# Sampled attention of a hybrid decoder step: the product with V, values held in the array and softmax weights streamed

## What is computed

```python
def diff_weights(logits, lam):
    p = jax.nn.softmax(logits, axis=-1)
    return p[:, :, 0] - lam * p[:, :, 1]

def sample_attn(q, k, v, lam, k_past, v_past, rel_bias):
    ...
    w = diff_weights(jnp.concatenate([s_past, s_new], axis=-1), lam).astype(v.dtype)
    return (jnp.einsum('bhqk,bkhe->bqhe', w[..., :past], v_past)
            + jnp.einsum('bhqk,bkhe->bqhe', w[..., past:], v))
```

## Time and profile before

| | us |
|---|---|
| median of three runs | 2044.64 |
| the profiled execution | 2045.42 |
| its span, first to last instruction | 2043.6 |
| third stage: its first key transposes to the last transposes of the norm | 835.6 to 1180.8 |
| one steady turn of it (8 heads' scores, one sequence's values) | 27.5 |

### The profile page before, as it was taken

One profiled execution on the slowest core, in us unless ns is written; L12 is line 12 of the kernel. 1 busy time (PEld: TensorE's weight loads), 2 busy tenths in 40 slices (PEclk: granted clock), 3 DMA queues, 4 the chain that ended last, 5 costly groups with the idle time before them and its releaser, 6 DMA issues. The chain is left out here.

```text
span 2043.6 us, 36009 instructions
## 1 busy us (share of the span) xinstructions
PE 1993.2 (98%) x11888; PEld 1850.2 (91%) x11888; DVE 1375.8 (67%) x2932; ACT 998.2 (49%) x1770; POOL 131.7 (6%) x158
## 2 busy tenths in 40 slices
PE   6999999999999999799999999999999999999998
PEld 6999999999999999688878799999999998989896
DVE  6766776767676767678785376675757474847476
ACT  5756575757565757677874242222313141313133
POOL 0000000000000000145560000000000000000000
PEclk9999999999999999999999999999999999999999
DMA  6411111112121112788873131111112020202012
GB/s 199 144 57 54 57 53 56 53 60 59 50 59 50 59 52 87 261 306 304 316 268 92 38 93 42 53 42 42 52 32 62 22 72 22 72 21 69 6 53 99
DMA packets 167453, 183.26 MB, mean 90 GB/s; under 512 B 11045, under 2 KB 139589, under 8 KB 167349
## 3 DMA queue, kind: packets, MB, share of 16 engines
q1 hardware_dynamic: 166137, 181.24, 27.1%
q10 hardware_dynamic: 1212, 0.81, 0.1%
HBM read 162.82 MB, written 24.46 MB: 92 GB/s over the span
## 5 line engine op out<-in xcount | busy, mean ns | idle before, releaser
L1250 PE MATMUL ps<-h_hi,w_hi 128*128 128x384 f32 (+1 forms) x1152 | 386.7, 336 | 5.0 <-DVEq L967 3.4
L1250 PE MATMUL ps<-h_hi,w_lo 128*128 128x384 f32 (+1 forms) x1152 | 376.5, 327 | 0.0
L1250 PE MATMUL ps<-h_lo,w_hi 128*128 128x384 f32 (+1 forms) x1152 | 376.4, 327 | 0.0
L2456 PE MATMUL ps<-h_hi,f_w_hi 128*128 128x320 f32 (+1 forms) x1136 | 370.7, 326 | 0.8 <-PEq L1579 0.8
L2456 PE MATMUL ps<-h_hi,f_w_lo 128*128 128x320 f32 (+1 forms) x1136 | 370.4, 326 | 0.0
L2456 PE MATMUL ps<-h_lo,f_w_hi 128*128 128x320 f32 (+1 forms) x1136 | 370.2, 326 | 0.0
L2535 ACT ACTIVATE yc<-ps,f_prm 128x384 f32<-128x384 f32 x144 | 93.5, 653 | 560.6 <-PE ps L2456 400.0
L2436 PE MATMUL ps<-d_hi,act 128*128 128x512 f32 x816 | 257.0, 390 | 0.5 <-issue 0.5
L1250 PEld LDWEIGHTS ps<-h_hi,w_hi 128*128 128x128 f32 x1152 | 217.0, 188 | 9.0 <-issue 4.0
L1250 PEld LDWEIGHTS ps<-h_lo,w_hi 128*128 128x128 f32 x1152 | 217.1, 188 | 0.6
L1250 PEld LDWEIGHTS ps<-h_hi,w_lo 128*128 128x128 f32 x1152 | 216.8, 188 | 0.0
(11 more groups left out here) (310 smaller groups left out, 3525.2 us busy)
## 6 DMA issues: line engine op xcount, KB each, us to landing
k<-in_cache_k SPq DMA_DIRECT2D x64, 512.0 KB, 5.9
v_raw<-in_cache_v SPq DMA_DIRECT2D x64, 512.0 KB, 4.7
w_raw<-in_w_in SPq DMA_DIRECT2D x48, 512.0 KB, 4.0
f_raw<-in_w_up SPq DMA_DIRECT2D x48, 512.0 KB, 4.0
f_raw<-in_w_down SPq DMA_DIRECT2D x24, 512.0 KB, 3.5
bias<-bias_tiles_dram SPq DMA_DIRECT2D x8, 576.0 KB, 3.6
merged_dram<-mg SPq DMA_DIRECT2D x8, 544.0 KB, 2.7
ow_raw<-in_w_out SPq DMA_DIRECT2D x8, 512.0 KB, 7.5
```

What stands on the lines that cost most here:

```text
L1250: last_ = pe.matmul(bank(s)[:, 0:n], w[:, W_SLOT[g], k, :], x[:, k, off:off + n], start=(k == 0 and i == 0), stop=(k == KT - 1 and i == 2))
L2456: l_ = pe.matmul(ps[:, e % 6, 0:n], w[:, p, k, :], x[:, k, off:off + n], start=(k == 0 and i == 0), stop=(k == KT - 1 and i == 2))
```

## The change

The two operands of the value product change places. For each page and each head the values of that head, v_hi and then v_lo (128 keys x 128 numbers), are the stationary operand, and the 16 columns of that head's weights (8 high, 8 low) move. A page is 16 matmuls of 16 columns instead of 4 of 512; the new tokens are 8 instead of 2. The result of a head is 128 numbers (partitions) x 16 columns, which is already the transposed, own block of each head: all of it is `own`, 128 columns of bank 7. `copy_o2`, `fold_heads`, their semaphores and `o2s` go; `fold_rows` reads `own` as soon as page 7 is done. `pt_both` is laid out head by head (8 high, 8 low columns of a head side by side), so that the copies and subtractions that fill it write runs of 8.

```diff
-    o2 = ps[:, 6:8, :].rearrange("p a n -> p (a n)")
+    own = ps[:, 7, 0:2 * NS]
...
-    pt_both = sb("pt_both", [128, NPAGES + 1, 2, NS], F32R, 158784)
-    o2s = sb("o2s", [128, D], F32, 163392)
+    pt_both = sb("pt_both", [128, NPAGES + 1, 2 * NS], F32R, 158784)
...
-    pt_hi, pt_lo = pt_both[:, :, 0, :], pt_both[:, :, 1, :]
+    pt_parts = pt_both[:, :, :].rearrange("p n (g a t) -> p (n g) a t", a=2, t=DEC_T)
+    pt_hi, pt_lo = pt_parts[:, :, 0, :], pt_parts[:, :, 1, :]
+    pt_rows = pt.rearrange("p (m t) -> p m t", t=DEC_T)
+    ptn_rows = ptn.rearrange("p (m t) -> p m t", t=DEC_T)
...
-            def fold_heads(count):
-
-                pe.wait_ge(o2_done, count)
-                pe.sem_inc(settled, 1)
-                for g in range(H):
-                    last = pe.transpose(o2[:, 128 * g:128 * (g + 1)], o2s[:, 128 * g:128 * (g + 1)], c.ident[:, :])
-                last.then_inc(ot_done, 1)
-
...
-                for hf in range(2):
-                    cols = slice(512 * hf, 512 * (hf + 1))
-                    parts = (v_hi[:, n, cols], v_lo[:, n, cols]) if n < NPAGES else (vn[:, cols],)
+                parts = (v_hi[:, n, :], v_lo[:, n, :]) if n < NPAGES else (vn[:, :],)
+                for g in range(H):
+                    cols = slice(2 * DEC_T * g, 2 * DEC_T * (g + 1))
                     for x, v in enumerate(parts):
-                        last = pe.matmul(o2[:, cols], pt_both[:, n, :, :].rearrange("p a n -> p (a n)"), v,
-                                         start=(n == 0 and x == 0), stop=(n == NPAGES - 1 and x == 1))
+                        last = pe.matmul(own[:, cols], v[:, 128 * g:128 * (g + 1)], pt_both[:, n, cols],
+                                         start=(n == 0 and g == 0 and x == 0),
+                                         stop=(n == NPAGES - 1 and g == H - 1 and x == 1))
...
-                    if h == 2 and has(b, 2):
-                        fold_heads(b - 1)
...
-                act.activation(o2s[:, :], o2, ACT.Copy).then_inc(o2_done, 1)
...
-                    if h == 1 and has(b, 2):
-                        copy_o2(b - 1)
...
-                dve.wait_ge(ot_done, b + 1)
+                dve.wait_ge(page_done, 8 * (b + 1))
                 dve.reduce_sum(oT[:, :, bass.ds(DEC_T * b, DEC_T)], own_rows, mybir.AxisListType.X)                   .then_inc(ots_done, 1)
```

More of the change, by code:

```diff
@@ L1470, in half_rows @@
         return hi, lo
-    own_rows = bass.AP(tensor=o2.tensor, offset=o2.offset,
-                       ap=[o2.ap[0], [128 + DEC_T, H], [1, DEC_T], [NS, 2]])
+    own_rows = bass.AP(tensor=own.tensor, offset=own.offset,
+                       ap=[own.ap[0], [2 * DEC_T, H], [1, DEC_T], [DEC_T, 2]])
     const_in = sem("s_const_in")
@@ L1500, in sampled_and_out @@
     page_done = sem("page_done")
-    o2_done = sem("o2_done")
-    ot_done = sem("ot_done")
     ots_done = sem("ots_done")
@@ L1865, in _ @@
             out_tile(0, range(4, KT))
-            fold_heads(DEC_B)
             out_tile(1, range(4, KT))
@@ L1927, in body @@
                         act.wait_ge(pt_done, b)
-                        act.activation(pt_hi[:, 0:NPAGES, :], pt.rearrange("p (n k) -> p n k", n=NPAGES), ACT.Copy)\
+                        act.activation(pt_hi[:, 0:H * NPAGES, :], pt_rows, ACT.Copy)\
                            .then_inc(pthi_done, 1)
-                        act.activation(pt_hi[:, NPAGES, :], ptn, ACT.Copy).then_inc(pthi_done, 1)
+                        act.activation(pt_hi[:, H * NPAGES:, :], ptn_rows, ACT.Copy).then_inc(pthi_done, 1)
                     if h == 0 and at_start(b):
@@ L1970, in _ @@
                 split_out("w", k)
-            copy_o2(DEC_B)
             act.wait_ge(ots_done, DEC_B)
@@ L2084, in body @@
                         dve.wait_ge(pthi_done, 2 * b)
-                        dve.tensor_tensor(pt_lo[:, 0:NPAGES, :], pt.rearrange("p (n k) -> p n k", n=NPAGES),
-                                          pt_hi[:, 0:NPAGES, :].bitcast(F32), ALU.subtract).then_inc(ptlo_done, 1)
-                        dve.tensor_tensor(pt_lo[:, NPAGES, :], ptn, pt_hi[:, NPAGES, :].bitcast(F32),
+                        dve.tensor_tensor(pt_lo[:, 0:H * NPAGES, :], pt_rows,
+                                          pt_hi[:, 0:H * NPAGES, :].bitcast(F32), ALU.subtract).then_inc(ptlo_done, 1)
+                        dve.tensor_tensor(pt_lo[:, H * NPAGES:, :], ptn_rows, pt_hi[:, H * NPAGES:, :].bitcast(F32),
                                           ALU.subtract).then_inc(ptlo_done, 1)
@@ L2729 @@
     "ktn_done slo_done s_sum_done s_vplo_done qdhi_done qdlo_done qkh_done s_ttr_done s_nmx_done s_exp_done c_done s_vhi_done s_vlo_done "
-    "new_hi new_lo pt_done pthi_done ptlo_done page_done o2_done ot_done ots_done s_sq_done s_ss_done "
+    "new_hi new_lo pt_done pthi_done ptlo_done page_done ots_done s_sq_done s_ss_done "
     "s_rst_done mgn_done s_settled s_chain s_achain ow_in0 ow_in1 o_raw_in0 o_raw_in1 "
```

## The result

| | before | after |
|---|---|---|
| median, us | 2044.78 (4 runs, 2043.51 to 2045.29) | 2154.65 (4 runs, 2152.91 to 2156.26) |
| ratio | | 1.0538, 95% interval 1.0520 to 1.0556 |
| the profiled execution, its span | 2045.42, 2043.6 | 2156.26, 2154.4 |
| mean granted clock over the span | 0.997 | 0.961 |
| a steady turn of the third stage | 27.5 | 40.1 to 42.2, mean of seven 41.2 |

The changed kernel is 110 us slower. That is the way that was forecast, and the time lies in the range of 2084 to 2180; but the likeliest case was 2092 us, a change of 48 us. It is within 3 us of the time that rival B gave, 2152.

The account below looks back on a forecast made before the run. PE's list of matmuls was taken to set the third stage's length. 2045.42 + 61.5 (pages) - 7.8 (fold) - 6 (waits) = 2093.1 us for the profiled execution, 0.8 above the median: 2092 us, range 2084 to 2180.

Parts of the forecast that it names:

- rival B: Third stage: few moving columns drop the clock to half in long stretches of pages, 60 us more, 2152 us; chance 0.36.
- case A: Likeliest case: all matmuls at the full clock, 0.115 us per page step, 2092 us, own range 2088 to 2105; chance 0.50.
- D: Rival: a weight load cannot start before the short matmul ahead is through, 0.19 us a step, 2174 us; chance 0.06.
- the 37 that it named as a sign of being wrong: Third stage: a turn was put at about 34.2 us; under 32 or over 37 would make the prediction wrong.
- PE was idle there: Argument against the clock falling: the earlier fall to 0.50 followed 3.4 us with PE busy for only 1.15.
- Part 1: Value product on PE: 272 matmuls at 0.234 us become 1088 at 0.115, 63.6 to 125.1 us, net +61.5.
- C: Rival: weight loads hide, steps under 0.07 us, kernel not slower, 2017 us at 0.045 a step; chance 0.05.
- E: Rival: short float32r matmuls are done in two passes, 2176 x 0.115 = 250 us, 2218 us in all; chance 0.03.
- Part 2: Removed copy of o2 and fold transposes: 1.03 us in each of 6 turns, about 0.8 in two, net -7.8 us.
- Part 3: PE's waits for key halves and POOL, and a clock fall, covered by longer pages: -6 us, at most 6.3.
- Part 4: Split of pt_both in runs of 8, later DVE sum and later value loads: costed at nothing.

Follow-up runs that it names:

- cols128: The changed kernel with all 128 weight columns of the page moving behind each weight load instead of the head's 16: 2087.26 us.
- fill8: The changed kernel, 16 columns per load, plus eight unused 512-column matmuls per page into a free bank: 2209.26 us.
- cols64: The changed kernel with 64 moving columns per weight load instead of 16, DVE's sum done in two instructions: 2131.24 us.
- fill4: The changed kernel, 16 columns per load, plus four unused 512-column matmuls per page into a free bank: 2210.80 us.
- nofold: The kernel before with its old value product, without the copy of o2 and the 8 transposes, the sum taken straight from o2: 2037.73 us.
- late: The kernel before, old product, with ACT's copy of o2 behind the keys of head 2 and the fold behind the key transposes at h = 3: 2044.28 us.
- spreadall: The changed kernel reordered as in spread, with the output projection's matmuls also put between the pages of the last turn: 2142.53 us.
- spread: The changed kernel, same instructions, with pages placed between the scores of heads instead of in long rows, last turn's pages still together: 2145.80 us.

## Why the prediction came out as it did

**Where the time went.** Seven turns from the first to the last weight transposition last 196.9 us before, 231.6 in cols128 and 288.3 after. Of the 67.4 us between cols128 and the change 56.7 lie in those turns and nearly all of the rest in the last one: its pages take 26.6 us (1160.12 to 1186.71) in place of 15.1.

**The step that failed is the weighing of rival B against case A.** The sum priced all matmuls at the full clock and had no term for its fall, because B was held less likely; the clock cost 67.4 us. Both cases' totals were near: A's 2092 against cols128's 2087, B's 2152 against 2155. B's was so in part by luck. It put 6.4 us at half the clock into each of seven turns and 15.6 into the last, 60 us in all; measured were 8.1 us a turn, since the clock was down for 17.1 to 20.5 us of each, scores and key transposes among them, and about 11 in the last, 67.4 in all. That B's price was 7 us too low is nearly hidden by A's sum, which was 5 us too high. B got 0.36, and the range was drawn so that B's upper part and D lay inside up to 2180; the measured time lies within that range, while the change itself, 110 us, is more than twice the 48 us that was forecast, and a turn of 41.2 us is over the 37 that it named as a sign of being wrong. Two sentences carried the choice. "PE was idle there, while here it never stops loading weights": PE was busy for all of every stretch and the clock fell. "Line 1777's stretch ran at the full clock": it did again after the change, but it stands between transposes and scores.

```profile
905.14 1.25 PE L1753 MATMUL ps<-ident,k 128*128 128x128 f32 x8
906.29 2.00 PE L1770 MATMUL ps<-C,P 128*128 128x64 f32 x16
908.12 0.39 PE L1775 MATMUL ps<-C,p_new 128*128 128x64 f32 x2
```

What the trace of before did hold was the other sentence, that 1.15 us of work was denser in columns than pages would be, and the runs bear it out as far as they go: with more columns moving, the clock held in cols128 and fill8 and fell less in cols64. A rule in columns alone does not order all runs (fill4 against cols64), and what exactly brings the clock down stays open. The Trainium skill ("TensorE: Matmul & The Clock Gate", The HAM clock gate) says that activity releases the throttle; the runs fit that, and weight loads with 16 columns behind each were not enough of it here.

**Part 1, the pages.** The step at the full clock was 0.112 us in place of 0.115: 1088 x 0.112 = 121.9, net 58.3 instead of 61.5. The nearest row, few columns behind a 128-column load, was the right one, and the 256-column row an upper bound as taken. Rivals C, D and E are out: no step near 0.07 or 0.19 at the full clock, and one instruction per matmul. C's 0.069 had come from transposes whose stationary operand is 64 x 64, half as many columns to load.

**Part 2, the fold.** 7.8 us predicted, 7.8 measured with the old product, about 6.5 with the new one, and 1.05 us in a steady turn with either, for 1.03. The mechanism held too: in nofold the key transposes start 1.59 us behind the start of the scores ahead instead of 2.64, where 1.61 was predicted (918.35 less 916.74). The wait recorded in front of them is 0.40 and not the 0.58 foretold: it is counted from the end of the scores' record, 1.19 us behind their start, where the prediction had PE free after 1.02. In late, where the copy stands behind the keys of head 2 and the transposes behind the wait, it is 0.40 too, so the copy's place ahead of the exponential did count.

**Part 3, waits.** At a held clock, cols128, the waits for key halves fell from 9.0 to 4.4 us, where 4.6 were to stay; POOL's 0.4 went, and the 0.6 for DVE's m_lo was 0.7 before; the fall of the clock at 1046 us, put at 1.5, went. That is 6.6 us, where 6 were taken and 6.3 were called the most. At the clock of the changed kernel the waits fell by more, and that was worth nothing.

**Part 4.** The split of the weights keeps its 0.69 and 0.21 us, and no wait for it appeared. The sum by parts at the full clock, 2045.4 + 58.3 - 7.8 - 6.6 = 2089.3, is 3 us above the profiled execution of cols128, 2086.42. The traces show where they are: single pages do not cost their number of steps. In a steady turn the pages last 8.3 us before, with a wait of 0.17 in it, and 15.0 in cols128, so 6.7 more, where 136 x 0.112 - 34 x 0.234 is 7.3; and 27.5 + 6.7 - 1.05 is 33.1, against 33.0 measured.

## What to carry to other kernels

Price an exchange of stationary and moving operand by the weight loads, not by the columns: with 128-column float32r loads, 16 and 128 moving columns cost the same 0.112 us here, and the saving has to come from elsewhere. Then ask what the clock will see: a list of matmuls that leaves PE no gap can still lose the upper clock level if little moves behind each load, and this cost more (67 us) than the matmuls themselves (58 us). Where loads are the bound, columns that nobody needs are free, and they can be worth having.

## What the hardware showed that was not expected

- The granted clock fell to 0.50 with PE busy for 3.40 of 3.40 us, for 7 to 10 us at a time, and 27.3 us in the last turn.
- 256 further matmuls of 512 columns, 58 us of work at the full clock, cost no time between fill4 (2210.80 us, clock 0.961) and fill8 (2209.26, 0.995).
- 128 instead of 16 moving columns behind each load took the kernel from 2154.65 to 2087.26 us.
- Executions differ more in forms where the clock falls in part of the turns or for unlike times in them: 16.5 us among four of cols64, 15.2 of fill4, 15.4 of spreadall and 6.3 of spread, against 2.1 of cols128 and 3.4 of the change.
- With pages between scores on both sides the clock was 1.00 in one turn of spread (878.4 to 888.6 us) and fell to 0.51 in the next (915.8 to 919.2).
